# Last feed forward: three projections on rows without the norm's root, the root applied to their outcome

## The chip, the cores and the metric

One Trainium2 chip, one of its cores. The time is the device time of one execution in microseconds (us). Engines: TensorE (PE in the rows, its weight loads PEld), VectorE (DVE), ScalarE (ACT), GpSimd (POOL), and SyncE (SP), which only issues DMAs.

## What is computed

Two transformer blocks in a row on 512 tokens of width 1024, in float32. The change lies at the very end, in layer 1 of the second block, between its attention and its last feed forward:

```
yx = ob.transpose(1, 0, 2, 3).reshape(B, S, H * Dh) @ wo            # attention's output projection
x = x + g_x * rmsnorm(yx, norm_g[i, 1])                             # post norm
fx = rmsnorm(x, norm_g[i, 2]) * (1.0 + scf_x) + shf_x               # norm ahead of the feed forward
x = x + gf_x * rmsnorm(swiglu(fx, ffn_w1[i], ffn_w3[i], ffn_w2[i]), norm_g[i, 3])

def rmsnorm(x, g):      x * rsqrt(mean(x * x) + EPS) * g            # the mean is over the 1024 features
def swiglu(h, w1, w3, w2):  (silu(h @ w1) * (h @ w3)) @ w2          # 2816 hidden features
```

`scf_x` (scale) and `shf_x` (shift) are vectors of 1024, the same for all tokens.

## The kernel before

Activations lie transposed: 128 features on the partitions, 512 tokens along the row, so a width of 1024 is `KD` = 8 chunks (`X[:, c, :]`). Each product is made of three float32r matmuls of a high and a low half (`three`, lines 443 to 445): Wh x Hh, Wh x Hl, Wl x Hh. A projection to 128 features is one "slab" of weights (1024 x 128, 512 KB) and 8 x 3 = 24 matmuls of 512 columns into one PSUM bank.

A slab goes through four hands. SyncE loads it into one of three `raw` buffers (L2719), once the low half of the slab three places earlier is done. ScalarE copies it into `Wh` (L2137), once the slab three places earlier has been used. Another engine subtracts to make `Wl`: VectorE (L1344), or GpSimd (L2647) for the slabs that `by_pool` names, all of the first block. ScalarE and VectorE do this inside `ahead(key)`, which prepares all slabs up to two behind `key`. Engines run their queues strictly in order, so what stands ahead of an `ahead` in the code delays it.

The stretch in question runs so:

- `gqa_attend`: eight slabs `wo2`. The sums of squares of their outcome `Y2` give the root of the post norm, per token, in a tiny tile `small`. `token_rows` transposes it to a row (L589), with keep-warm matmuls around it (L651: float32 matmuls whose outcome nobody reads, `fill_in` gives their numbers, 1 and 4).
- `post_norm`: for each chunk VectorE scales `Y2` by gain and root (L1441) and adds it to `X` (L1512). ScalarE squares the new `X` (L2172), TensorE sums the squares over the partitions with a float32 matmul against ones (`norm_stat`, L565), eight times, and eight keep-warm matmuls follow.
- `norm_to_h`: ScalarE takes logarithm and exponential (L2185, L2188), VectorE refines the root with four operations (`rstd`, L1414, L1417, L1419, L1423; the result is `stat_r`, called `SR`), and then for each chunk VectorE scales `X` by gain and root (L1441), ScalarE adds the shift and writes the high half `Hh` (L2210), VectorE writes the low half `Hl` (L1458).
- `ffn_2`: for f = 0 to 10, and later 11 to 21, the projections `up1` and `up3` of hidden chunk f. The first two run together, chunk by chunk as `Hl` appears (`linear_pair`); the others one after the other (`linear`). ScalarE takes SiLU of up1 out of PSUM into `sl` (L2157), VectorE multiplies by up3 (L1673), ScalarE writes the high half `g_h` (L2307), VectorE the low half `g_l` (L1500). After 11 of them come the down projections.

In the text the projections are numbered in the order in which TensorE does them: up1 f=0, up3 f=0, up1 f=1, up3 f=1 (the fourth), up1 f=2 (the fifth).

Of the kernel before, what the change touches and what calls it, by code (L numbers as in the profile page):

```python
# [24 lines left out]
P = 128  # L25
# [69 lines left out]
def write(nc, a, out, tally):  # L95
# [197 lines left out]
    Y2 = at("Y2", 32, [KD, SEQ])  # L293
    XT = nc.alloc_sbuf_tensor_at("XT", [P, QT, D], F32, offset=int(hl_base - 16 * KB))
# [88 lines left out]
    WARM = 8  # L383

    def by_pool(key):

        return key[0] in BLOCK_1_SLABS or key[0:2] == ("dn", 1)
# [18 lines left out]
    def _(pe):  # L406
# [50 lines left out]
        def linear(job, key, src, n):  # L457
# [4 lines left out]
            gemm(job, w, Hh, Hl, n).then_inc(*fill(job))  # L462
            release[key] = full(job)
            mods()
# [91 lines left out]

        def stat(job, parts, n, matrix="ones"):
# [80 lines left out]
        WARM_AFTER = {("n1", 0): WARM, ("ln", "c"): 4, ("f", 0, "c"): 4, ("n", 1, "c"): 4, ("f", 1, "x"): WARM}  # L638
# [139 lines left out]
        def ffn_2(l, s):  # L778

            n, tag = NS[s], ("f", l, s)  # L780
            for half in range(2):
                for f in range(half * FH, (half + 1) * FH):
                    w = {x: a["ffn_w%s_2" % x][l, :, f * P:(f + 1) * P] for x in "13"}
                    if f == 0:
                        linear_pair(tag, n, *((("up" + x, l, s, f), w[x], "split") for x in "13"))
                    else:
                        for x in "13":
                            linear(("up" + x, l, s, f), ("up" + x, l, s, f), w[x], n)
# [374 lines left out]
        def gqa_attend():  # L1163
# [63 lines left out]
            token_rows(("post", ("att", "x")), fill_in=(1, 4))  # L1227
# [64 lines left out]
        pre(("f", 1, "x"), SEQ)  # L1292
# [23 lines left out]
    def _(dve):  # L1316
# [343 lines left out]

        def ffn_2(l, s):
            n, tag = NS[s], ("f", l, s)
            name = ("dn", 2, l, s)
            norm_to_h(tag, n, lambda c: col(2, l, s, 7, c), lambda c: col(2, l, s, 3, c))
            for half in range(2):
                for f in range(half * FH, (half + 1) * FH):
                    u1, u3 = ("up1", l, s, f), ("up3", l, s, f)
                    ahead(u1)
                    ahead(u3)
                    dve.wait_ge(*free(u1))  # L1670
                    dve.wait_ge(*full(u3))
                    i, o = tmp((name, f))
                    dve.tensor_tensor(o[:, 0:n], sl[f % 2][:, 0:n], bank(u3, n), ALU.mult).then_inc(*empty(u3))  # L1673
# [440 lines left out]
        post_norm(("att", "x"), SEQ, Y2, lambda c: col(2, 1, "x", 8, c))  # L2114
# [3 lines left out]
    def _(act):  # L2118
# [190 lines left out]
        def ffn_2(l, s):  # L2309
            n, tag, name = NS[s], ("f", l, s), ("dn", 2, l, s)  # L2310
            norm_to_h(tag, n, lambda c: col(2, l, s, 3, c))
            for half in range(2):
                for f in range(half * FH, (half + 1) * FH):
                    u1, u3 = ("up1", l, s, f), ("up3", l, s, f)
                    ahead(u1)
                    if f >= 2:
                        act.wait_ge(*free(("up3", l, s, f - 2)))
                    evict(u1, sl[f % 2][:, 0:n], n, ACT.Silu)
                    ahead(u3)
                    act.wait_ge(*free(u3))  # L2320
# [313 lines left out]
        squares_of_x(("f", 1, "x"), SEQ, lambda c: ready("x_new", ("att", "x"), c))  # L2634
# [183 lines left out]
```

## Time and profile before

| | us |
|---|---|
| median of 3 runs | 3263.64 |
| lowest and highest | 3260.55, 3272.95 |
| profiled execution | 3269.63 |
| its span in the trace | 3267.7 |
| TensorE busy in it | 3154.4 (97%) |
| VectorE, ScalarE, GpSimd busy | 1568.1, 1185.1, 817.0 |

The span is the trace's own; the profiled execution's time is 1.9 us more. Times in the rows count from the start of the span. The stretch that the change touches lies between 2866 and about 2911.

### The profile page before, as it was taken

How to read it: one execution, taken by the hardware profiler on the slowest of the kernel's cores; microseconds unless marked ns; L12 is line 12 of the kernel's file. 1: busy time of each engine (PE TensorE's matmuls, PEld its weight loads, DVE VectorE, ACT ScalarE, POOL GpSimd, SP SyncE). 2: the span in 40 equal slices, each digit the busy share in tenths (PEclk: the TensorE clock that was granted, in tenths of full speed). 3: DMA queues.
4: the chain of work that ended last, by engine and by line, in shares of the span. 5: the costliest groups of instructions: out<-in, count | busy, mean ns of one | idle time of the engine just before them, and what ended most of it. 6: DMA issues, size and time to landing. Idle time of an engine off the chain costs nothing.

```text
span 3267.7 us, 38743 instructions
## 1 busy us (share of the span) xinstructions
PE 3154.4 (97%) x15600; PEld 2489.3 (76%) x15600; DVE 1568.1 (48%) x2210; ACT 1185.1 (36%) x1764; POOL 817.0 (25%) x401
## 2 busy tenths in 40 slices
PE   6999999999999999999999899999999979999998
PEld 4657778887665777778877678888888658878887
DVE  3572146465366113334289754322334889653234
ACT  3443234243453224324331343121112558632223
POOL 4302436565330433344411000000000039400000
PEclk9999999999999999999999899999999989999999
DMA  6413426755430555463335212212221110122332
GB/s 238 126 46 109 139 88 191 227 181 179 123 118 12 161 178 170 149 192 91 94 97 131 54 49 61 65 60 64 65 65 52 43 35 1 40 71 87 107 89 79
DMA packets 429894, 337.23 MB, mean 103 GB/s; under 512 B 16638, under 2 KB 411224, under 8 KB 417429
## 3 DMA queue, kind: packets, MB, share of 16 engines
q1 hardware_dynamic: 427888, 333.42, 33.3%
q8 instruction: 125, 2.05, 0.3%
q10 hardware_dynamic: 580, 0.88, 0.1%
q0 software_dynamic: 1248, 0.46, 0.1%
q14 instruction: 53, 0.43, 0.0%
HBM read 319.58 MB, written 2.10 MB: 98 GB/s over the span
## 4 chain that ended last, share of the span: by engine, by line
PE 62%; DVE 5%; issue 1%; ACT 1%; SPq 0%; DMA 0%; ACTq 0%; POOL 0%; DVEq 0%
PE PS L443 18%; PE PS L444 17%; PE PS L445 17%; PE PS L902 1%; PE PS L577 1%; PE PS L1206 1%; PE PS L651 1%; PE PS L565 1%; PE PS L1175 1%; PE PS L696 1%; PE PS L1207 1%; PE PS L1186 1%; DVE X L1512 0%; PE PS L1176 0%; DVE q_parts L1783 0%
## 5 line engine op out<-in xcount | busy, mean ns | idle before, releaser
L443 PE MATMUL PS<-Hh,Wh 128*128 128x512 f32 x2208 | 875.4, 396 | 7.8 <-DVE Hl L1458 7.8
L2647 POOL TENSOR_TENSOR Wl<-raw,Wh 128x1024 fp32r<-128x1024 f32 (+2 forms) x254 | 617.2, 2438 | 992.5 <-ACT Wh L2137 992.5
L444 PE MATMUL PS<-Hl,Wh 128*128 128x512 f32 x2208 | 861.8, 390 | 0.0
L445 PE MATMUL PS<-Hh,Wl 128*128 128x512 f32 x2208 | 861.1, 390 | 0.0
L2137 ACT ACTIVATE Wh<-raw 128x1024 fp32r<-128x1024 f32 (+2 forms) x442 | 435.9, 987 | 394.0 <-PE PS L445 346.8
L443 PEld LDWEIGHTS PS<-Hh,Wh 128*128 128x128 f32 x2208 | 415.7, 188 | 115.7 <-issue 50.5
L445 PEld LDWEIGHTS PS<-Hh,Wl 128*128 128x128 f32 x2208 | 415.7, 188 | 87.5
L444 PEld LDWEIGHTS PS<-Hl,Wh 128*128 128x128 f32 x2208 | 416.1, 188 | 69.0 <-issue 3.7
L1344 DVE TENSOR_TENSOR Wl<-raw,Wh 128x1024 fp32r<-128x1024 f32 (+3 forms) x188 | 217.5, 1157 | 380.6 <-ACT Wh L2137 380.1
L2042 DVE SCALAR_TENSOR_TENSOR cv<-PS,vcols,cv 128x510 f32<-128x510 f32 (+1 forms) x176 | 123.7, 745 | 216.9 <-ACT cv L2566 216.9
L443 PE MATMUL PS<-g_h,Wh 128*128 128x512 f32 x528 | 206.6, 391 | 3.5 <-POOL Wl L2647 3.5
L2679 POOL CAST k_hi<-k_ctx 64x512 fp32r<-64x512 f32 x4 | 4.2, 1042 | 806.2 <-DVE k_ctx L1441 806.0
L445 PE MATMUL PS<-g_h,Wl 128*128 128x512 f32 x528 | 205.5, 389 | 0.0
L444 PE MATMUL PS<-g_l,Wh 128*128 128x512 f32 x528 | 205.5, 389 | 0.0
L444 PE MATMUL PS<-hc_l,Wh 128*128 128x256 f32 x576 | 161.9, 281 | 0.0
L445 PE MATMUL PS<-hc_h,Wl 128*128 128x256 f32 x576 | 161.8, 281 | 0.0
L443 PE MATMUL PS<-hc_h,Wh 128*128 128x256 f32 x576 | 161.8, 281 | 0.0
L2694 POOL TENSOR_SCALAR p<-p,small 128x768 f32<-128x768 f32 x64 | 140.4, 2214 | 49.7 <-DVE small L2094 49.7
L2566 ACT ACTIVATE cv<-PS,vcols 128x512 f32<-128x512 f32 x88 | 68.6, 780 | 192.2 <-PE PS L445 188.8
L565 PE MATMUL PS<-sq,cst 128*128 128x512 f32 (+2 forms) x196 | 100.4, 627 | 26.5 <-DVE stat_v L1414 16.2
L443 PEld LDWEIGHTS PS<-hc_h,Wh 128*128 128x128 f32 x576 | 108.1, 188 | 19.7
L444 PEld LDWEIGHTS PS<-hc_l,Wh 128*128 128x128 f32 x576 | 108.1, 188 | 19.7
(390 smaller groups left out, 4806.1 us busy)
## 6 DMA issues: line engine op xcount, KB each, us to landing
raw<-in_ffn_w SPq DMA_DIRECT2D x108, 512.0 KB, 3.6
mod_w<-in_w_mod SPq DMA_DIRECT2D x48, 1024.0 KB, 4.9
raw<-in_w_up SPq DMA_DIRECT2D x88, 512.0 KB, 4.7
mod_w<-in_w_ada SPq DMA_DIRECT2D x40, 1024.0 KB, 4.8
raw<-in_w_in SPq DMA_DIRECT2D x62, 512.0 KB, 3.9
raw<-in_w_down SPq DMA_DIRECT2D x32, 384.0 KB, 4.9
raw<-in_conv_w_pw SPq DMA_DIRECT2D x24, 512.0 KB, 4.1
UQ<-U SPq DMA_DIRECT2D x112, 99.4 KB, 2.2
```

The lines of the kernel that those rows point to most:

```text
L443: pe.matmul(o, wh, xh, start=start, stop=False, skip_group_check=True)
L444: pe.matmul(o, wh, xl, start=False, stop=False, skip_group_check=True)
L445: return pe.matmul(o, wl, xh, start=False, stop=stop, skip_group_check=True)
L565: mm = pe.matmul(bank(job, n), const(matrix)[lo:hi, :], SQ[i][lo:hi, 0:n], start=first, stop=final, skip_group_check=True)
L577: mm = pe.matmul(PS[:, bank_of[job], t:t + 1], part[:, t * P:(t + 1) * P], const("ones", 0, 1), start=first and t == 0, stop=final, skip_g ...
L651: pe.matmul(PS[:, b, :], const("ident"), cst[:, 0:512], start=True, stop=True)
L1344: dve.tensor_tensor(low, src, high.bitcast(F32), ALU.subtract).then_inc(*mark("w_low", k))
L2042: ins = dve.scalar_tensor_tensor(o, bank(ups[s])[:, 0:SEQ - lag], vec(("w_conv", l), tap * 2 * FC + s * FC + f), o, ALU.mult, ALU.add)
L2137: act.activation(high, src, ACT.Copy).then_inc(*mark("w_high", k))
L2566: act.activation(cv[f % 2][s][:, :], bank(job), ACT.Identity, bias=vec(("b_conv", l), s * FC + f), scale=vec(("w_conv", l), 2 * 2 * FC + s ...
L2647: pool.tensor_tensor(low, src, high.bitcast(F32), ALU.subtract).then_inc(*mark("w_low_pool", one[0]))
L2694: pool.tensor_scalar(p2[n % 5][:, :], p2[n % 5][:, :], ri2[n % 5], None, ALU.mult)\
```

## The change

Three slabs are "late": up1 f=0, up3 f=0, up1 f=1. They no longer read `Hh` and `Hl`, but `late_h` and `late_l`, the halves of x times gain without root and shift. The root is one factor per token, so it can be applied to the outcome; the shift's share is one number per hidden feature, which 24 one-column matmuls of the raw weights against the shift vector give. The fourth and all later projections read `Hh` and `Hl` as before, the fourth chunk by chunk. The low halves of the slabs of the third, fourth and fifth projection are made by GpSimd. `post_norm_late` is `post_norm` with the late low half two chunks behind.

The diff, cut to its core, in the order TensorE (`linear_late`), VectorE (`post_norm_late` and the first `ffn_2`), ScalarE (the second `ffn_2`), GpSimd, SyncE (the wait ahead of the fourth projection's load):

```diff
+    LATE = ("up1", 1, "x", 0), ("up3", 1, "x", 0), ("up1", 1, "x", 1)
+    LATE_LOWS = ("up1", 1, "x", 1), ("up3", 1, "x", 1), ("up1", 1, "x", 2)
     def by_pool(key):
-        return key[0] in BLOCK_1_SLABS or key[0:2] == ("dn", 1)
+        return key[0] in BLOCK_1_SLABS or key[0:2] == ("dn", 1) or key in LATE_LOWS
...
+        def linear_late(tag, srcs):
...
+            for m, job in enumerate(LATE):
+                r = (first + m) % RAW
+                pe.wait_ge(*ready("raw_in%d" % r, job))
+                for i in range(KD):
+                    mm = pe.matmul(PS[:, bank_of[shift], m:m + 1], raw[r][:, i * P:(i + 1) * P],
+                                   MOD[2, 1][:, 3 * KD + i, 0:1], start=(m, i) == (0, 0), stop=i == KD - 1,
+                                   skip_group_check=True)
+            mm.then_inc(*fill(shift))
...
+            for i in range(KD):
+                norm_stat(tag, i, n)
+                pe.wait_ge(*ready("late_low", tag, i))
+                for job, w in zip(LATE, ws):
+                    mm = products(job, w, i)
...
+            job, w = LATE[2], slab(LATE[2], k_p(srcs[2]), KD, P)
+            for i in range(KD):
+                mm = products(job, w, i)
...
-        WARM_AFTER = {("n1", 0): WARM, ("ln", "c"): 4, ("f", 0, "c"): 4, ("n", 1, "c"): 4, ("f", 1, "x"): WARM}
+        WARM_AFTER = {("n1", 0): WARM, ("ln", "c"): 4, ("f", 0, "c"): 4, ("n", 1, "c"): 4}
...
-            token_rows(("post", ("att", "x")), fill_in=(1, 4))
+            token_rows(("post", ("att", "x")), fill_in=(1, 1))
-        pre(("f", 1, "x"), SEQ)
...
+        def post_norm_late(tag, post, n, src, gg, g):
...
+            def low(c):
+                dve.wait_ge(*ready("late_high", tag, c))
+                dve.scalar_tensor_tensor(late_l[c][:, 0:n], x[:, c, 0:n], g(c), late_h[:, c, 0:n].bitcast(F32),
+                                         ALU.mult, ALU.subtract).then_inc(*mark("late_low", tag, c))
...
         def ffn_2(l, s):
...
+            dve.wait_ge(*full(("shift", tag)))
+            dve.tensor_copy(shift_out, PS[:, bank_of["shift", tag], 0:3]).then_inc(*empty(("shift", tag)))
...
+                    if u1 in LATE:
+                        dve.wait_ge(*full(u1))
+                        dve.tensor_tensor(late_o[:, 0:n], bank(u1, n), SR[:, 0:n], ALU.mult).then_inc(*empty(u1))
...
+                    if u3 in LATE:
...
+                        dve.scalar_tensor_tensor(o[:, 0:n], late_o[:, 0:n], shift_out[:, 1:2], sl[f % 2][:, 0:n],
+                                                 ALU.add, ALU.mult).then_inc(*mark("late_gate", f))
...
         def ffn_2(l, s):
...
-            norm_to_h(tag, n, lambda c: col(2, l, s, 3, c))
+            ahead(first_slab(tag))
+            for c in range(KD):
+                act.wait_ge(*ready("x_new", ("att", "x"), c))
+                act.activation(late_h[:, c, :], X[:, c, :], ACT.Identity, scale=DER[2, l][:, KD + c, 0:1])\
+                   .then_inc(*mark("late_high", tag, c))
+                square((tag, c), X[:, c, 0:n], n)
+            root(("ss", tag), n)
+            ahead(LATE[1])
...
+            norm_highs(tag, n, lambda c: col(2, l, s, 3, c))
...
+                    if u1 in LATE:
+                        act.wait_ge(*free(u1))
+                        silu(sl[f % 2][:, 0:n], tb(("late", u1))[:, 0:n], bias=shift_out[:, 2 * f:2 * f + 1])\
+                            .then_inc(*mark("late_silu", f))
...
+        for key in LATE_LOWS:
...
+            pool.wait_ge(*ready("w_high", key))
+            pool.tensor_tensor(low, src, high.bitcast(F32), ALU.subtract).then_inc(*mark("w_low_pool", key))
...
+                if slabs[n - RAW][0] == LATE[0]:
+                    sp.wait_ge(*full(("shift", LATE_TAG)))
```

TensorE, from the transposes of the post norm's root on, before:

```order
L589 MATMUL PS<-cst,small 128x128 x4
L651 MATMUL PS<-cst 128x512 x4
L565 MATMUL PS<-sq0,cst 128x512
L565 MATMUL PS<-sq1,cst 128x512
...
L651 MATMUL PS<-cst 128x512 x8
L443 MATMUL PS<-Hh,Wh0 128x512
L444 MATMUL PS<-Hl,Wh0 128x512
```

and now (L694 and L632 are the old L651 and L589, L608 the old L565, L451 to L453 the old L443 to L445):

```order
L632 MATMUL PS<-cst,small 128x128 x4
L694 MATMUL PS<-cst 128x512
L577 MATMUL PS<-mod2_1,raw0 128x1 x8
L577 MATMUL PS<-mod2_1,raw1 128x1 x8
L577 MATMUL PS<-mod2_1,raw2 128x1 x8
L608 MATMUL PS<-sq0,cst 128x512
L451 MATMUL PS<-late_h_159,Wh0 128x512
L452 MATMUL PS<-late_l0_160,Wh0 128x512
L453 MATMUL PS<-late_h_159,Wl0 128x512
L451 MATMUL PS<-late_h_159,Wh1 128x512
L452 MATMUL PS<-late_l0_160,Wh1 128x512
L453 MATMUL PS<-late_h_159,Wl1 128x512
```

Eleven keep-warm matmuls are gone, 24 one-column ones are there, and each statistic is followed by six products.

ScalarE, from the end of the norm's highs on (`Wh1` behind `g_h` is the fifth projection's weights in both), before:

```order
L2210 ACTIVATE Hh<-tmp0,mod2_1 128x512
L2157 ACT_TABLE_LOAD
L2157 ACTIVATE sl0_118<-PS 128x512
L2137 ACTIVATE Wh0<-raw0 128x1024
L2307 ACTIVATE g_h_112<-tmp1 128x512
L2137 ACTIVATE Wh1<-raw1 128x1024
L2157 ACTIVATE sl1_119<-PS 128x512
```

and now:

```order
L2301 ACTIVATE Hh<-tmp0,mod2_1 128x512
L2241 ACT_TABLE_LOAD
L2241 ACTIVATE sl0_118<-tmp1,mod_row_52 128x512
L2398 ACTIVATE g_h_112<-tmp0 128x512
L2228 ACTIVATE Wh1<-raw1 128x1024
L2241 ACTIVATE sl1_119<-tmp1,mod_row_52 128x512
```

The fourth projection's weights (`Wh0`) have moved ahead of the highs; the fifth's stand where they stood, behind `g_h`.

VectorE, from the end of the norm's lows on, before:

```order
L1458 SCALAR_TENSOR_TENSOR Hl<-tmp0,mod2_1,Hh 128x512
L1344 TENSOR_TENSOR Wl2<-raw2,Wh2 128x1024
L1344 TENSOR_TENSOR Wl0<-raw0,Wh0 128x1024
L1673 TENSOR_TENSOR tmp1<-sl0_118,PS 128x512
L1500 TENSOR_TENSOR g_l_113<-tmp1,g_h_112 128x512
```

and now (`mod_row` holds the shift's share):

```order
L1501 SCALAR_TENSOR_TENSOR Hl<-tmp0,mod2_1,Hh 128x512
L1739 COPY mod_row_52<-PS 128x3
L1748 TENSOR_TENSOR tmp1<-PS,stat_r 128x512
L1754 TENSOR_TENSOR tmp2<-PS,stat_r 128x512
L1760 SCALAR_TENSOR_TENSOR tmp0<-tmp2,mod_row_52,sl0_118 128x512
L1543 TENSOR_TENSOR g_l_113<-tmp0,g_h_112 128x512
```

Three low halves of weights have gone to GpSimd, and a copy, the products with the root and a gate that adds the shift's share have come.

## Rows read from the trace of the kernel before

**Rows 1.** The page's chain that ended last, shares of the span by engine.

```profile
PE 62%; DVE 5%; issue 1%; ACT 1%; SPq 0%; DMA 0%; ACTq 0%; POOL 0%; DVEq 0%
```

**Rows 2.** Busy times by stretch: length, PE, PEld, DVE, ACT, POOL; clock; DMA.

```profile
2870.00:2880.00 10.00, 9.46 (x20) 3.01 (x18) 9.97 (x16) 4.15 (x7) 0.00 (x0) 1.00 0.00 0
...
2900.00:2912.00 12.00, 12.00 (x55) 9.93 (x54) 5.66 (x6) 4.33 (x7) 0.00 (x0) 1.00 0.57 166
```

**Rows 3.** TensorE's timeline: start, us, line, out<-in, count [idle before]; two rows per float32 matmul.

```profile
2866.06 0.95 PE L577 MATMUL PS<-cst,stat_v 128*128 128x1 f32 x8
2866.91 1.05 PE L577 MATMUL PS<-cst,sq 128*128 128x1 f32 x8
...
2869.76 3.60 PE L651 MATMUL PS<-cst 128*128 128x512 f32 x8
2873.20 9.10 PE L565 MATMUL PS<-sq,cst 128*128 128x512 f32 x16
2882.13 7.03 PE L651 MATMUL PS<-cst 128*128 128x512 f32 x16
2888.60 0.79 PE L443 MATMUL PS<-Hh,Wh 128*128 128x512 f32 x1
...
2910.56 0.39 PE L445 MATMUL PS<-Hh,Wl 128*128 128x512 f32 x1
2910.78 0.39 PE L443 MATMUL PS<-Hh,Wh 128*128 128x512 f32 x1
```

**Rows 4.** VectorE's timeline in the same stretch.

```profile
2870.03 1.41 DVE L1441 SCALAR_TENSOR_TENSOR tmp<-Y,der,PS 128x512 f32<-128x512 f32 x2 [0.87 <-PE PS L589]
2871.35 0.69 DVE L1512 TENSOR_TENSOR X<-X,tmp 128x512 f32<-128x512 f32 x1
...
2887.57 0.75 DVE L1458 SCALAR_TENSOR_TENSOR Hl<-tmp,mod,Hh 128x512 fp32r<-128x512 f32 x1 [0.19 <-ACT Hh L2210]
...
2897.07 1.22 DVE L1344 TENSOR_TENSOR Wl<-raw,Wh 128x1024 fp32r<-128x1024 f32 x1
...
2902.15 0.68 DVE L1673 TENSOR_TENSOR tmp<-sl,PS 128x512 f32<-128x512 f32 x1
```

**Rows 5.** ScalarE's timeline in the same stretch.

```profile
2872.07 0.63 ACT L2172 ACTIVATE sq<-X 128x512 f32<-128x512 f32 x1 [3.57 <-DVE X L1512]
...
2882.33 0.69 ACT L2185 ACTIVATE stat_y<-PS,cst 128x512 f32<-128x512 f32 x1 [1.43 <-PE PS L565]
...
2883.59 1.04 ACT L2137 ACTIVATE Wh<-raw 128x1024 fp32r<-128x1024 f32 x1
...
2902.86 0.63 ACT L2307 ACTIVATE g_h<-tmp 128x512 fp32r<-128x512 f32 x1 [1.89 <-DVE tmp L1673]
2903.40 1.04 ACT L2137 ACTIVATE Wh<-raw 128x1024 fp32r<-128x1024 f32 x1
```

**Rows 6.** Timeline of GpSimd and VectorE in the first block, a low half alone last.

```profile
126.65 2.74 POOL L2647 TENSOR_TENSOR Wl<-raw,Wh 128x1024 fp32r<-128x1024 f32 x1 [5.71 <-ACT Wh L2137]
...
127.18 2.77 DVE L1423 SCALAR_TENSOR_TENSOR stat_r<-stat_t,stat_y 128x512 f32<-128x512 f32 x1
...
1080.61 2.39 POOL L2647 TENSOR_TENSOR Wl<-raw,Wh 128x1024 fp32r<-128x1024 f32 x1 [4.23 <-ACT Wh L2137]
```

**Rows 7.** The page's DMA issues of feed forward slabs: count, size, median us to landing.

```profile
raw<-in_ffn_w SPq DMA_DIRECT2D x108, 512.0 KB, 3.6
```

**Rows 8.** Busy times by stretch again, two places where the clock fell.

```profile
46.00:50.00 4.00, 4.00 (x12) 3.10 (x12) 4.00 (x7) 2.20 (x4) 0.00 (x0) 0.58 0.10 29
...
1844.00:1848.00 4.00, 4.00 (x25) 4.00 (x24) 4.00 (x10) 1.89 (x3) 0.00 (x0) 0.59 0.00 0
```

**Rows 9.** TensorE's timeline at these two places.

```profile
44.76 0.77 PE L443 MATMUL PS<-Hh,Wh 128*128 128x512 f32 x1 [5.25 <-DVE Hl L1458]
...
49.71 0.40 PE L443 MATMUL PS<-Hh,Wh 128*128 128x512 f32 x1
...
1843.21 17.07 PE L577 MATMUL PS<-cst,sq 128*128 128x1 f32 x85 [1.10 <-ACT sq L2172]
```

More of the change, by code:

```diff
@@ L455, in gemm, with linear @@
             return mm
-        def linear(job, key, src, n):
+        def linear(job, key, src, n, each=None):
             begin(job)
@@ L461, in linear @@
             tally.h_reader[0] = job
-            gemm(job, w, Hh, Hl, n).then_inc(*fill(job))
+            gemm(job, w, Hh, Hl, n, each=each).then_inc(*fill(job))
             release[key] = full(job)
@@ L784, in ffn_2 @@
                     if f == 0:
[L785 removed]
+                        linear_late(tag, [w["1"], w["3"], a["ffn_w1_2"][l, :, P:2 * P]])
                     else:
[L787 to L788 removed]
+                        for x in "13"[f == 1:]:
+                            linear(("up" + x, l, s, f), ("up" + x, l, s, f), w[x], n,
+                                   each=(lambda i: ready("h_low", tag, i)) if f == 1 else None)
                 down(("dn", 2, l, s), a["ffn_w2_2"][l], half, n, None, last_turns)
@@ L1659, in ffn_both, with add @@
             post_norms(("ffn", 0), 0, 9)
+        def post_norm_late(tag, post, n, src, gg, g):
+            row, x, pending = ("r", ("post", post)), X, []
+            dve.wait_ge(*full(row))
+            def add(c, i, t):
+                dve.wait_ge(*t)
+                tmp_free[i] = after(dve.tensor_tensor(x[:, c, 0:n], x[:, c, 0:n], TMP[i][:, 0:n], ALU.add),
+                                    "x_new", post, c)
+            def low(c):
+                dve.wait_ge(*ready("late_high", tag, c))
+                dve.scalar_tensor_tensor(late_l[c][:, 0:n], x[:, c, 0:n], g(c), late_h[:, c, 0:n].bitcast(F32),
+                                         ALU.mult, ALU.subtract).then_inc(*mark("late_low", tag, c))
+            for c in range(KD + 2):
+                if c < KD:
+                    i, o = tmp(("post", post, c))
+                    t = scaled(o[:, 0:n], src[:, c, 0:n], gg(c), n, r=bank(row, n))
+                    if c < KD - 1:
+                        t = own(t)
+                    else:
+                        t.then_inc(*empty(row))
+                        t = free(row)
+                    pending.append((c, i, t))
+                if 0 < c <= KD:
+                    add(*pending[c - 1])
+                if c > 1:
+                    low(c - 2)
         def ffn_2(l, s):
@@ L2695, in _ @@
                 .then_inc(*mark("p2_scaled", h, i))
+        for key in LATE_LOWS:
+            d = [one[0] for one in slabs].index(key)
+            src, high = halves(slabs[d], raw[d % RAW], Wh[d % WS])
+            _, low = halves(slabs[d], raw[d % RAW], Wl[d % WS])
+            pool.wait_ge(*ready("w_high", key))
+            pool.tensor_tensor(low, src, high.bitcast(F32), ALU.subtract).then_inc(*mark("w_low_pool", key))
     @block.sync
```

49 lines of the change are left out of this document (40 added, 9 removed).

## The prediction, made before the change was run

> **What bounds the kernel now.** I read the chain that ended last first [rows 1]: matmuls carry most of it, and VectorE is next. So a change pays only where TensorE waits or runs filler. The change touches one such place, the stretch between the attention's output projection and the fifth projection of the last feed forward; I read it in the busy times by stretch [rows 2] and then instruction by instruction. TensorE looks full there, but look at what it does [rows 3]: statistics and keep-warm matmuls (L651) fill it from 2869.76 to 2888.60. The first projection starts at 2888.60, when VectorE hands over the first low part. From then on nothing stops: four projections are 96 matmuls, the last of them issues at 2910.56, and the fifth projection starts at 2910.78, so a matmul of 512 columns costs 0.227 us and a projection 5.44. Everything behind the fifth projection is fed in time in both kernels, so the change is worth what it does to this 2910.78.
>
> **The change, part by part.**
>
> TensorE first. One keep-warm matmul remains after the row transposes instead of four: four take 3.44 us (2869.76 to 2873.20), so one ends at 2870.62 [rows 3]. Now 24 one-column matmuls for the shift follow. The nearest rows are the one-column ones of L577: eight trace rows in 0.85 us, and eight rows are four float32 matmuls (the program order says x4), so 0.213 us each and 5.1 us for 24. They end at 2875.8 (rounded up for the change of form). The first statistic would be ready at about 2873.4: ScalarE's first square starts at 2872.07 [rows 5], and the new high part, 0.6 to 0.7, goes ahead of it. So the shift's matmuls are exposed by 2.4 us.
>
> Then come eight rounds of one statistic, 0.86 (the price of a float32 matmul of 512 columns), and six products, 1.36: 2.22 us a round. VectorE's round is 0.66 + 0.60 + 0.66 = 1.9 us (row gain and sum in [rows 4], and a third operation of the form of L1458), ScalarE's two activations are 1.2, so TensorE sets the pace. The low part of chunk 0 is due at 2874.0, or 0.7 later if it meets GpSimd; TensorE wants it at 2876.7. The last statistic ends at T = 2875.8 + 7 x 2.22 + 0.86 = 2892.2. Before, T was 2882.13 (the next matmul's start in [rows 3]). T is 10.1 us later, and two projections lie ahead of it instead of behind. The third follows with no wait and ends at T + 1.36 + 5.44 = T + 6.8.
>
> The root and the eight chunks of the norm are the same work as before. From T to the end of the last low part it took 2897.07 - 2882.13 = 14.9 us [rows 3, 4]. What is new is GpSimd beside it. ScalarE converts the fourth projection's weights at the same point as before, 1.3 us behind its logarithm [rows 5]; the low half that follows is now GpSimd's. In [rows 6] such a low half started during L1419, and the next VectorE operation, the same L1423 with two SBUF operands, took 2.77 us instead of 0.69. The timing here would be the same within 0.2 us. I take the whole 2.08: the norm ends at T + 17.0. Bounds: 0 (no meeting) and 2.4 (a full GpSimd operation, [rows 6]).
>
> The fourth projection reads this norm chunk by chunk; chunk 0 comes at T + 8.3, chunk 7 at T + 17.1, and it ends at T + 17.9. TensorE works there half the time.
>
> Then the point on which the forecast turns. In the order of ScalarE, the conversion of the fifth projection's weights stands behind sl0 and g_h of f = 0, and these wait for VectorE, which does them only when its norm is over. Before, that conversion began at 2903.40 [rows 5] and with VectorE's low half (1.2) was done five microseconds early. Now the chain from the end of the norm is: shift copy 0.3, product with the root 0.7, SiLU 0.65, gate 0.7 to 0.75 (with the waits between them 2.45 up to the start of g_h), g_h 0.54 and the conversion 1.05 [rows 5], GpSimd's low half 0.1 + 2.39 [rows 6], and 0.1 to the matmul: 6.6 us. On VectorE a low half took 1.2; on GpSimd it is twice that. The fifth projection starts at T + 17.0 + 6.6 = T + 23.6 = 2915.8 against 2910.78: **5.0 us later**. TensorE stands still for 5.7 us ahead of it.
>
> No other queue comes into it. SyncE holds the fourth projection's load until the shift's matmuls are over (2875.8), and the two loads queued behind it wait too; three loads of 3.6 us [rows 7] end by about 2887, and the first is wanted at T + 1.5. The eight VectorE operations added in the post norm (5.3 us) are covered by TensorE's slower round; that cover is 0.3 us a chunk and would cost 0.3 x 8 if it were gone. The three scalings by the root and the SiLU on a scaled copy are in the chain above for f = 0 and behind the fifth projection's matmuls for f = 1.
>
> **The clock.** Two new places look like ones where the granted clock fell. First, one-column matmuls: at 1843.21 a long row of them starts right behind 512-column work; in 1844 to 1848 the clock is 0.59 though TensorE is busy all the time [rows 8, 9], which is a mix of 2.4 and 1.2 GHz. Here 5.2 us of them come behind a stretch that is already thin. I take 5 us at 1.2 GHz, which cost half, 2.5 us (bounds 0 and 3.4); T and all behind it move by that. The Trainium skill ("TensorE: Matmul & The Clock Gate", section "Why this matters for your kernels") says otherwise: it advises to keep TensorE continuously busy to have the full clock, and by that the one-column matmuls, issued without a gap, would protect it. By the skill's rule the term is 0 and the sum 2.5 us lower; the trace does not agree, since the rows show the clock falling in a full queue. Second, the pause of 5.7 us: behind one of 5.25 us, twelve matmuls took 4.95 us (44.76 to 49.71) instead of 2.7, and the clock of 46 to 50 is 0.58 [rows 8, 9]. That is 2.2 us (bounds 1.5 and 3.4).
>
> **Sum:** 5.0 + 2.5 + 2.2 = 9.7 us slower. The profiled execution took 3269.63 us (span 3267.7), so its like would be 3279.3; it stood 6.0 above the median of the runs shown, which gives 3263.64 + 9.7 = **3273.3 us**. That is 0.3%. About 0.5% (16.3 us) is what a measurement of this kernel can tell from no change, so I call it the same, with the sign on the slow side.
>
> **Rivals.** (1) The clock holds through one or both places. For it: TensorE has had fillers in this stretch with the clock at 1.00 throughout [rows 2]. Against it: [rows 8, 9]. Time: +5.0 to +7.5, 3268.6 to 3271.1. (2) The early part is cheap: the one-column matmuls end before the first square is ready (they would have to take under 0.12 us each), which gives 2.4 back, the clock stays up, and GpSimd and VectorE do not meet, another 2.1: 5.0 - 4.5 = +0.5, 3264.1. Only if GpSimd's low half were as quick as VectorE's besides (1.2 less) would the change be ahead, by 0.7 us. For it: the new form has no row of its own, and the square of chunk 0 could come later than I say, behind its high part. Against it: each of the terms has a row. The change's own aim, projections ahead of the root, is limited by the fourth projection in any case: it cannot end before the norm does, T + 15.8. With the cheap T of 2889.8 that is 2905.6, a gain of 5 us if the fifth projection's weights were ready, which the order excludes. (3) Slower beyond 0.5%: the clock stays at 1.2 GHz for long. The thin stretch begins at 2866, the half-busy fourth projection and the pause follow, and in the one-column stretch of [rows 9] (17 us) the clock did not come back while it lasted. If it stayed low from the shift's matmuls to behind the pause, the dense rounds would run at half speed. It decides from (16.3 - 5.0) x 2 = 23 us of dense work at 1.2 GHz; for 26 us it gives +18, 3282. Against it: eight rounds of six full products are dense, and after the pause at 44.76 the full clock was back at 49.71.
>
> **How the numbers follow.** The forecast as summed, between +7.5 and +13: 0.62. Rival 1: 0.20. Rival 2, with any smaller time, gains included: 0.09. Rival 3: 0.09. Unknown costs from their bounds give -2.1 to +0.3 (port), -2.5 to +0.9 (first clock term), -0.7 to +1.2 (second); the runs before lie from 3260.55 to 3272.95, so a median can move by 4 for no reason. From rival 1 less that to the forecast's upper end plus that: 3264 to 3284. I take 3263 to 3284. Faster by over 0.5% would need more than the whole stretch holds: 0.01. Slower by over 0.5% is rival 3: 0.09. The rest, 0.90, lies within.
>
> **What the changed profile would show.** 24 one-column matmuls (48 rows) from about 2870.6, over 5 us long; rounds of 2.2 us; the last statistic at about 2892 to 2895; L1466 (stat_r) at about 2.8 us beside GpSimd's low half; the fourth projection in eight pieces 1.3 us apart; a pause of nearly 6 us ended by GpSimd's Wl; the fifth projection 23.6 us behind the last statistic; and a granted clock under 1 in two places. I am wrong if the fifth projection starts before 2911, if the pause is not there, if L1466 stays at 0.69, or if the clock stays at 1.00 from 2870 to 2920.

## The result, and the profile after

The changed kernel took **3275.65 us** (median of 20 runs, 3269.96 to 3284.09), the kernel before 3264.95 us on the same chip (20 runs, 3259.91 to 3273.09). The medians differ by 10.7 us. The ratio is 1.0029 with a 95% interval of 1.002 to 1.0039, which is a cost of 6.5 to 12.7 us. The forecast was 9.7 us and 3273.3 us.

The page barely shows it. The chain that ended last is the one of [rows 1] with a point moved from VectorE to issue:

```profile
PE 62%; DVE 4%; issue 2%; ACT 1%; SPq 0%; DMA 0%; POOL 0%; ACTq 0%; POOLq 0%; DVEq 0%
```

The profiled execution took 3271.65 us (span 3269.8), only 2.0 more than the one before. The rest lies ahead of the change: this execution reached the token sums that open the touched stretch at 2857.62, the one before at 2866.06 [rows 3], 8.4 us later, though the program is the same up to there. So totals of single executions say nothing here, and I count everything from the start of these token sums. Seen from there, the product that VectorE forms behind the sixth projection (the gate of f = 2, the first step that both kernels have alike) starts at 66.39 us in the changed kernel and at 55.86 in the one before: **10.53 us later**. The next ones are 10.2, 10.5 and 10.5 later. The whole loss is in this stretch: from the token sums to the end of the span it is 412.2 us against 401.7, the same 10.5 that the gate shows. 10.53 - 8.44 = 2.1 is what the two profiled executions differ by (2.0), and 10.53 lies within the interval of the timing.

TensorE's timeline in the stretch (start and length in us, count, idle before in brackets), to be laid beside [rows 3]:

```profile
2862.18 5.50 PE L577 MATMUL PS<-mod,raw 128*128 128x1 f32 x48
2867.55 2.06 PE L608 MATMUL PS<-sq,cst 128*128 128x512 f32 x2
...
2873.68 1.02 PE L608 MATMUL PS<-sq,cst 128*128 128x512 f32 x2
...
2875.92 1.02 PE L608 MATMUL PS<-sq,cst 128*128 128x512 f32 x2
```

```profile
2894.18 0.47 PE L451 MATMUL PS<-Hh,Wh 128*128 128x512 f32 x1 [1.40 <-DVE Hl L1501]
...
2910.55 0.79 PE L451 MATMUL PS<-Hh,Wh 128*128 128x512 f32 x1 [6.67 <-POOL Wl L2806]
2911.14 0.63 PE L452 MATMUL PS<-Hl,Wh 128*128 128x512 f32 x1
2911.57 0.63 PE L453 MATMUL PS<-Hh,Wl 128*128 128x512 f32 x1
```

The first row is the shift's share, 24 matmuls of one column in 5.37 us. Behind it come the eight rounds, 2.24 us from one statistic (L608) to the next. The first of them reads 2.06 instead of 1.02. Then the fourth projection in eight pieces, and the row to look at longest: the fifth projection starts at 2910.55, after 6.67 us in which TensorE does nothing, released by GpSimd's low half. Its first matmuls take 0.63 instead of the 0.39 of [rows 3].

Busy times by stretch (columns as in [rows 2]: PE, PEld, DVE, ACT, POOL; clock; DMA):

```profile
2866.00:2871.00 5.00, 5.00 (x22) 3.63 (x22) 5.00 (x9) 2.49 (x5) 0.00 (x0) 0.66 0.40 116
2871.00:2886.00 15.00, 15.00 (x55) 9.95 (x53) 6.81 (x11) 5.65 (x10) 0.00 (x0) 1.00 0.22 67
...
2906.00:2910.00 4.00, 0.00 (x0) 0.00 (x0) 1.76 (x3) 3.03 (x4) 1.85 (x1) 0.79 0.01 2
2910.00:2914.00 4.00, 3.45 (x8) 2.77 (x9) 2.80 (x4) 1.79 (x3) 0.50 (x1) 0.50 0.53 154
2914.00:2918.00 4.00, 4.00 (x16) 3.21 (x16) 1.04 (x1) 0.00 (x0) 0.00 (x0) 0.86 0.79 231
```

The clock fell twice, as in [rows 8]: once while TensorE was busy all the time (first row; 0.66 over 5 us is 3.4 us at 1.2 GHz), and once in the pause and on into the fifth projection (0.50 from 2910 to 2914).

What TensorE waited for stands in the timelines of VectorE, ScalarE and GpSimd, which answer [rows 4 to 6]:

```profile
2888.87 2.77 DVE L1466 SCALAR_TENSOR_TENSOR stat_r<-stat_t,stat_y 128x512 f32<-128x512 f32 x1
...
2901.23 1.63 DVE L1501 SCALAR_TENSOR_TENSOR Hl<-tmp,mod,Hh 128x512 fp32r<-128x512 f32 x2
2902.78 0.15 DVE L1739 COPY mod_row<-PS 128x3 f32<-128x3 f32 x1
2902.85 0.68 DVE L1748 TENSOR_TENSOR tmp<-PS,stat_r 128x512 f32<-128x512 f32 x1
...
2905.71 0.75 DVE L1760 SCALAR_TENSOR_TENSOR tmp<-tmp,mod_row,sl 128x512 f32<-128x512 f32 x1 [1.59 <-ACT sl L2241]
```

```profile
2885.97 0.69 ACT L2276 ACTIVATE stat_y<-PS,cst 128x512 f32<-128x512 f32 x1 [3.86 <-PE PS L608]
...
2903.61 1.28 ACT L2241 ACT_TABLE_LOAD   x1 [1.53 <-DVE tmp L1748]
2904.90 0.72 ACT L2241 ACTIVATE sl<-tmp,mod_row 128x512 f32<-128x512 f32 x1
2906.50 0.63 ACT L2398 ACTIVATE g_h<-tmp 128x512 fp32r<-128x512 f32 x1 [0.88 <-DVE tmp L1760]
2907.03 1.04 ACT L2228 ACTIVATE Wh<-raw 128x1024 fp32r<-128x1024 f32 x1
```

```profile
2888.34 2.74 POOL L2806 TENSOR_TENSOR Wl<-raw,Wh 128x1024 fp32r<-128x1024 f32 x1 [24.90 <-ACT Wh L2228]
2908.15 2.35 POOL L2806 TENSOR_TENSOR Wl<-raw,Wh 128x1024 fp32r<-128x1024 f32 x1 [17.06 <-ACT Wh L2228]
```

Read the last four rows of ScalarE and the second of GpSimd as one chain: product with the root at 2902.85, **table load at 2903.61**, SiLU, gate, g_h, conversion, low half, and TensorE at 2910.55. The load is the one link that the prediction doesn't have. In the kernel before, the same load runs ahead of any wait, three microseconds before its SiLU's products are there:

```profile
2896.39 1.28 ACT L2157 ACT_TABLE_LOAD   x1
2899.43 0.60 ACT L2157 ACTIVATE sl<-PS 128x512 f32<-128x512 f32 x1 [1.76 <-PE PS L445]
```

A product of VectorE ahead of the SiLU isn't enough to hold the load. In the first block of the changed kernel the load ran ahead of such a wait:

```profile
473.10 1.28 ACT L2241 ACT_TABLE_LOAD   x1
474.56 0.63 ACT L2241 ACTIVATE sl<-cv 128x512 f32<-128x512 f32 x1 [0.17 <-DVE cv L2133]
```

The code has one wait in front of the SiLU at both of these places, and two at 2903.61 (for the shift copy and for the product). That the second wait is what keeps the load behind fits these rows, but no run tests it.

### The profile page after: what moved, and what is told of

It reads as the page before. It is cut to its first block, busy times and chain, and to the rows that moved or that the text cites. A ratio compares the mean times of both kernels' runs of the same rounds, so it can differ in the third digit from the quotient of the medians.

```text
span 3269.8 us, 38816 instructions
## 1 busy us (share of the span) xinstructions
PE 3143.6 (96%) x15626; PEld 2484.2 (76%) x15626; DVE 1575.0 (48%) x2219; ACT 1190.6 (36%) x1772; POOL 824.9 (25%) x404
## 4 chain that ended last, share of the span: by engine, by line
PE 62%; DVE 4%; issue 2%; ACT 1%; SPq 0%; DMA 0%; POOL 0%; ACTq 0%; POOLq 0%; DVEq 0%
PE PS L451 17%; PE PS L452 17%; PE PS L453 17%; PE PS L946 1%; PE PS L620 1%; PE PS L1250 1%; PE PS L1219 1%; PE PS L739 1%; PE PS L608 1%; PE PS L1251 1%; PE PS L1230 1%; PE PS L694 1%; PE PS L1220 0%; DVE q_parts L1874 0%; DVE both_tmp L1484 0%
## 5 line engine op out<-in xcount | busy, mean ns | idle before, releaser
L451 PE MATMUL PS<-Hh,Wh 128*128 128x512 f32 x2184 | 867.1, 397 | 18.2 <-DVE Hl L1501 11.4
L452 PE MATMUL PS<-Hl,Wh 128*128 128x512 f32 x2184 | 852.8, 390 | 0.0
L453 PE MATMUL PS<-Hh,Wl 128*128 128x512 f32 x2184 | 852.4, 390 | 0.0
L451 PEld LDWEIGHTS PS<-Hh,Wh 128*128 128x128 f32 x2184 | 411.6, 188 | 128.6 <-issue 52.5
L453 PEld LDWEIGHTS PS<-Hh,Wl 128*128 128x128 f32 x2184 | 411.3, 188 | 87.2
L451 PE MATMUL PS<-g_h,Wh 128*128 128x512 f32 x528 | 206.7, 391 | 3.5 <-POOL Wl L2752 3.5
L453 PE MATMUL PS<-g_h,Wl 128*128 128x512 f32 x528 | 205.5, 389 | 0.0
L453 PE MATMUL PS<-hc_h,Wl 128*128 128x256 f32 x576 | 161.8, 281 | 0.0
L451 PE MATMUL PS<-hc_h,Wh 128*128 128x256 f32 x576 | 161.8, 281 | 0.0
L2799 POOL TENSOR_SCALAR p<-p,small 128x768 f32<-128x768 f32 x64 | 140.7, 2220 | 49.7 <-DVE small L2185 49.7
L608 PE MATMUL PS<-sq,cst 128*128 128x512 f32 (+2 forms) x196 | 98.0, 606 | 26.8 <-DVE stat_v L1457 16.2
L451 PEld LDWEIGHTS PS<-hc_h,Wh 128*128 128x128 f32 x576 | 108.1, 188 | 19.7
```

What stands on the lines that cost most here:

```text
L451: pe.matmul(o, wh, xh, start=start, stop=False, skip_group_check=True)
L452: pe.matmul(o, wh, xl, start=False, stop=False, skip_group_check=True)
L453: return pe.matmul(o, wl, xh, start=False, stop=stop, skip_group_check=True)
L608: mm = pe.matmul(bank(job, n), const(matrix)[lo:hi, :], SQ[i][lo:hi, 0:n], start=first, stop=final, skip_group_check=True)
L2799: pool.tensor_scalar(p2[n % 5][:, :], p2[n % 5][:, :], ri2[n % 5], None, ALU.mult)\
```

## The experiments

Two theories stood at the start. **Mine:** four separate costs make up the 10.5 us, which are the shift's matmuls with the clock that they bring down, GpSimd's low half in VectorE's way, the chain from the norm's end to the fifth projection's weights (with the table load in it), and the clock behind the pause. **The rival:** one of them makes the others (the pause is there anyway, since the sixth projection or the norm ends last), so that mending one moves nothing. All numbers of this table are from the traces, in us from the start of the token sums; "log" is the start of the post norm's logarithm (L2276), which starts 0.2 behind the last statistic, "gate" the gate of f = 2.

| kernel | log | root's widest operation | fifth projection | gate | log to gate | half clock ahead of log / at the fifth or sixth |
|---|---|---|---|---|---|---|
| before | 16.27 | 0.69 | 44.72 | 55.86 | 39.6 | none / none |
| changed | 28.35 | 2.77 | 52.93 | 66.39 | 38.0 | 3.4 / 6.8 |
| table load early | 29.98 | 2.77 | 53.28 | 66.27 | 36.3 | 6.8 / 6.8 |
| filler in the pause | 29.94 | 2.76 | 54.60 | 65.88 | 35.9 | 6.8 / none |
| narrow low half | 31.57 | 0.83 | 54.21 | 67.18 | 35.6 | 10.2 / 6.8 |
| fifth's weights early | 28.34 | 2.77 | 48.1 | 63.42 | 35.1 | 3.4 / 3.4 |
| 3 of 24 shift matmuls | 24.65 | 2.77 | 49.24 | 62.72 | 38.1 | none / 6.8 |
| shift matmuls spread | 27.97 | 2.77 | 52.57 | 66.10 | 38.1 | none / 6.8 |
| four queue edits | 28.34 | 0.69 | 45.49 | 56.90 | 28.6 | 3.4 / none |
| the same, spread 9 + 15 | 27.96 | 0.69 | 45.11 | 56.50 | 28.5 | none / none |
| the same, spread 15 + 9 | 26.67 | 0.69 | 43.83 | 55.21 | 28.5 | none / none |

The stretch ahead of the logarithm and the one behind it hang on different things, and the length of the first half clock changed from run to run of the same code (below). So an edit behind the logarithm is read from the column "log to gate". The totals of the single executions (3271.2 to 3276.1 us for the first four variants, 3280.0, 3283.2 and 3274.0 for the next three) are not used: the latter three had reached the token sums only at 2869.6, 2869.6 and 2868.7, 11 to 12 us later than the changed kernel, ahead of any edit.

**The table load ahead of the wait.** ScalarE loads the SiLU table before it waits for VectorE's product:

```diff
+                        if table_set[0] != SILU:
+                            act.preload_act_table_set(SILU)
+                            table_set[0] = SILU
                         act.wait_ge(*free(u1))
```

> The change with one edit: ScalarE loads the SiLU table before it waits for VectorE's product with the root, not after it. All times from the start of the post norm's one-column sums. In the changed kernel the fifth projection starts at 52.9 us and the gate of f = 2 (the end of the sixth projection) runs at 66.4 (before the change: 44.7 and 55.9). Theory A (the fifth projection's weights wait behind VectorE's norm and ScalarE's sl0 and g_h, so every step of that chain counts): the load of 1.28 us lies in the chain, and hiding it gives 1.1 to 1.3: fifth at 51.7, gate at 65.2. Theory B (the late root alone sets the time, and the chain has slack): no change, 52.9 and 66.4.

The load ran beside the norm's last chunk, and the pause became shorter by its length (ScalarE's and TensorE's timelines):

```profile
2902.81 1.28 ACT L2420 ACT_TABLE_LOAD   x1
2904.34 0.72 ACT L2241 ACTIVATE sl<-tmp,mod_row 128x512 f32<-128x512 f32 x1 [0.25 <-DVE tmp L1748]
```

```profile
2909.99 0.80 PE L451 MATMUL PS<-Hh,Wh 128*128 128x512 f32 x1 [5.39 <-POOL Wl L2809]
```

5.39 instead of 6.67: the load costs 1.28 us, all of its length, in the chain. From the logarithm to the gate it is 1.75: the second half clock reached 3.5 us into the fifth projection here and 4.6 in the changed kernel, which is the other 0.5. The Trainium skill ("ScalarE: Activation LUTs", section "Step-by-step: what each stage is for") says that the compiler places such a load right before the activation that needs it; this trace agrees, and here that place is behind the wait, while in the kernel before it was ahead of it (2896.39 and 2899.43 above). (The section "What ACT_TABLE_LOAD costs" gives about 1283 ns for the load, as measured here, and 1380 ns of drain besides, which isn't in these rows: the SiLU follows the load at once, and taking the load away gave 1.28 and not 2.7.)

**Filler in the pause.** Six keep-warm matmuls ahead of the fifth projection:

```diff
+                            if f == 1 and x == "3":
+                                keep_warm(6)
```

> The change with six keep-warm matmuls (5.2 us) between the fourth and the fifth projection, where TensorE stands still for 6.7 us. Theory A (the pause makes the clock fall, and that costs 2.3 us of the fifth projection): the fifth still starts at 52.9, its matmuls run at 2.4 GHz, the gate of f = 2 comes 2.2 us earlier, at 64.2. Rival (the clock falls because of what was ahead: the half-busy fourth projection, or at random): clock under 1 in the fifth projection all the same, gate at 66.4.

The idle time ahead of the fifth projection fell to 1.61 us and its matmuls ran at full clock:

```profile
2913.00:2918.00 5.00, 4.95 (x22) 4.14 (x23) 3.51 (x4) 1.58 (x2) 0.00 (x0) 1.00 0.71 208
```

The fifth projection started no earlier (24.66 behind the logarithm, 24.58 in the changed kernel), and the gate was 2.1 us nearer. That is the price of the second half clock, forecast at 2.2.

**A narrow low half.** GpSimd makes only 128 of the 1024 columns of the fourth projection's low half (the rest is left out):

```diff
-            pool.tensor_tensor(low, src, high.bitcast(F32), ALU.subtract)
+            cols = slice(0, P) if key == LATE_LOWS[1] else slice(0, 8 * P)
+            pool.tensor_tensor(low[:, cols], src[:, cols], high[:, cols].bitcast(F32), ALU.subtract)
```

> The change with GpSimd's low half of the fourth projection's weights made for 128 of 1024 columns only (the rest is left out, so the fourth projection is computed with old low halves there). Theory A (GpSimd's operation blocks VectorE's stat_r, 2.77 instead of 0.69 us): stat_r at 0.7 to 1.0, the norm and with it the fifth projection 1.8 to 2.1 us earlier, at 50.9, gate of f = 2 at 64.4. Rival (VectorE's operation is long by itself, or waits for ScalarE): stat_r stays near 2.8, nothing moves.

```profile
2893.99 0.83 DVE L1466 SCALAR_TENSOR_TENSOR stat_r<-stat_t,stat_y 128x512 f32<-128x512 f32 x1
```

```profile
2893.46 0.82 POOL L2807 TENSOR_TENSOR Wl<-raw,Wh 128x128 fp32r<-128x128 f32 x1 [28.13 <-ACT Wh L2228]
```

VectorE's operation was 0.83 beside a short GpSimd operation and 2.77 beside a long one, with the same operands: it waits for GpSimd to end. The fifth projection came 1.94 us nearer to the logarithm, and the pause stayed 6.67, so this cost (2.08 forecast) adds to the pause and isn't part of it. (The gate came 2.4 us nearer. The other 0.5 is again the second half clock, which reached 3.6 us into the fifth projection instead of 4.6.) The Trainium skill ("SBUF — State Buffer", section "SBUF: two separate sides") has this as a lock that whichever of the two starts first holds for its whole instruction. The rows agree: GpSimd's 2888.34 + 2.74 is 2891.08, and VectorE's operation, put at 2888.87, ended at 2891.64, a normal operation's 0.6 behind that.

**The fifth projection's weights early.** ScalarE converts them right behind the logarithm, where the fourth's are converted:

```diff
-            ahead(LATE[1])
+            ahead(LATE[2])
```

> The change with the conversion of the fifth projection's weights moved on ScalarE from behind g_h of f = 0 to ahead of the norm's highs, next to the fourth's. Theory A (this place in ScalarE's order makes the pause; GpSimd's second low half now blocks one more VectorE operation for about 2.4 us): pause gone, fifth at 48.4, straight behind the fourth, no fall of the clock there, gate of f = 2 at 59.5. The same without a second block: 46.0 and 57.1. Theory B (the late root alone): the fifth stays at 52.9.

The fifth projection came where I had it, right behind the fourth. The gate was four microseconds later than expected, for the next row of TensorE's timeline is a new wait:

```profile
2917.79 0.39 PE L453 MATMUL PS<-Hh,Wl 128*128 128x512 f32 x1
2920.48 0.47 PE L451 MATMUL PS<-Hh,Wh 128*128 128x512 f32 x1 [2.30 <-DVE Wl L1387]
```

The sixth projection's conversion now stood where the fifth's had, behind sl1 on ScalarE (2918.03), and TensorE waited for that with another half clock behind it. And GpSimd made two low halves in a row, which held VectorE twice:

```profile
2895.21 5.53 POOL L2806 TENSOR_TENSOR Wl<-raw,Wh 128x1024 fp32r<-128x1024 f32 x2 [24.89 <-ACT Wh L2228]
```

```profile
2895.74 2.77 DVE L1466 SCALAR_TENSOR_TENSOR stat_r<-stat_t,stat_y 128x512 f32<-128x512 f32 x1
2898.55 3.40 DVE L1484 SCALAR_TENSOR_TENSOR tmp<-X,der,stat_r 128x512 f32<-128x512 f32 x2
```

So the rival holds in part: the gate gained 2.9 us (35.1 behind the logarithm instead of 38.0), and the rest of the wait went to the next conversion in the line.

**Three of the 24 one-column matmuls.** The loop over the chunks runs for the last one only:

```diff
-                for i in range(KD):
+                for i in range(KD - 1, KD):
```

> Of the 24 one-column matmuls for the shift's share only the last chunk's 3 are left (the rest of the share is not computed). Times here are from the start of the token sums. In the changed kernel the fifth float32 row of filler and the 24 matmuls were followed by 3.41 us at the half clock, and the post norm's logarithm began at 28.35 (29.9 in two variants in which the half clock lasted 6.83 us). My theory: the full queue of one-column matmuls makes the clock fall and they are exposed by about 2.4 us; with 3 of them both are gone: no stretch of half clock before the post norm, logarithm at about 24.0 (28.35 - 2.4 - 1.9). Rival: the clock falls anyway, for the thin work of the token sums and the filler ahead of them, and the matmuls cost only their exposure: half clock is still there near 9 to 10, logarithm at 25.7 or later. The rest of the stretch moves with the logarithm: fifth projection 24.6 behind it by both.

The half clock ahead of the logarithm was gone, and TensorE waited 2.50 us for the first square:

```profile
2874.20 0.72 PE L577 MATMUL PS<-mod,raw 128*128 128x1 f32 x6
2877.43 1.10 PE L608 MATMUL PS<-sq,cst 128*128 128x512 f32 x2 [2.50 <-ACT sq L2263]
```

The logarithm came at 24.65 (24.0 expected): 3.7 us earlier. If 1.7 of it is the clock (3.4 us at half of it), 2.0 is left for the time by which 21 matmuls ran past the first square. Behind the logarithm nothing changed (38.1).

**The same 24, spread.** 9 ahead of the rounds, 3 behind each of five rounds:

```diff
-                for i in range(KD):
-                    mm = pe.matmul(PS[:, bank_of[shift], m:m + 1], raw[r][:, i * P:(i + 1) * P],
+            def shifts(i):
+                for m in range(3):
+                    mm = pe.matmul(PS[:, bank_of[shift], m:m + 1], raw[(first + m) % RAW][:, i * P:(i + 1) * P],
...
+            for i in range(3):
+                shifts(i)
...
+                if i + 3 < KD:
+                    shifts(i + 3)
```

> The same 24 one-column matmuls, but 9 ahead of the eight rounds and 3 behind the statistic and the products of each of the first five rounds; nothing is left out. My theory: it is the unbroken row of them that makes the clock fall, so the half clock of 3.41 or 6.83 us near 9.7 is gone (1.7 to 3.2 us), the logarithm begins at about 26.6 instead of 28.35, and the rounds that carry three more are 0.65 us longer than the others (2.24). Rival: their number is what counts, or the thin work around them: half clock near 9 to 11 stays, logarithm at 28.3 or 30.

No half clock, as expected; but the logarithm came at 27.97 and not at 26.6. The expected 26.6 is 28.35 less the clock's 1.7, with the matmuls exposed no more than before (2.0 us). But the fifteen in the rounds cost their full length, 5 x 0.67 = 3.3 us on top of the 24.65 with three, since TensorE sets the pace of the rounds; and 1.16 us ahead of the first square stayed empty.

**Four queue edits together.** VectorE makes the low halves of the fourth and fifth projections (right behind the root and right behind the norm), ScalarE converts the fifth's weights ahead of the norm and the sixth's behind its last high part, and loads the table early:

```diff
-    LATE_LOWS = ("up1", 1, "x", 1), ("up3", 1, "x", 1), ("up1", 1, "x", 2)
+    LATE_LOWS = (("up1", 1, "x", 1),)
...
-            norm_to_h(tag, n, lambda c: col(2, l, s, 7, c), lambda c: col(2, l, s, 3, c))
+            rstd(("ss", tag), n, D)
+            ahead(LATE[1])
+            norm_to_h(tag, n, lambda c: col(2, l, s, 7, c), lambda c: col(2, l, s, 3, c), rooted=True)
+            ahead(LATE[2])
...
-            ahead(LATE[1])
+            ahead(LATE[2])
...
+            ahead(("up3", l, s, 1))
```

> Four edits of the queues, nothing of the computation: VectorE in place of GpSimd makes the low halves of the fourth projection (right behind the root) and of the fifth (right behind the norm); ScalarE converts the fifth's weights ahead of the norm's last steps and the sixth's behind them; and ScalarE loads the SiLU table ahead of its wait for VectorE's product. My theory: each wait that the four looks so far found has gone and no other takes its place: the widest operation of the root is 0.7 instead of 2.77, the norm is shorter by 2.1 less the 1.2 of the low half that VectorE now makes in it, the fifth projection begins about 17.3 behind the logarithm (24.58 in the changed kernel), the sixth follows without the 2.30 that it waited in the look before, and the gate of f = 2 starts about 28.3 behind the logarithm (38.0). With the logarithm at 28.3 to 30 that is 56.6 to 58.3 behind the token sums (66.4 in the changed kernel, 55.9 in the one before). Rival: a new wait comes up, on the bank of the third f's products or on VectorE's queue, and the gate stays 33 or more behind the logarithm, near the 35.1 of the early fifth.

From the logarithm to the gate it was 28.56 us (28.3 expected, 38.0 in the changed kernel): 9.5 us are mended by these four edits. The second half clock is gone with the pause, and no new wait came up: the longest on TensorE from the fourth projection to the gate is 0.50 us. The four were not taken apart here. TensorE's row at the fifth projection:

```profile
2914.16 0.49 PE L451 MATMUL PS<-Hh,Wh 128*128 128x512 f32 x1 [0.17 <-DVE Wl L1387]
```

**The edits and the spread together**, timed against the kernel before:

> The four edits of the queues and the spread one-column matmuls together. By my theory it keeps the change's idea and loses what cost it: logarithm at 26.6, gate of f = 2 at 54.8 behind the token sums against 55.9 in the kernel before, so a time 1 us below before, 3264 (3260 to 3268), which is the same by any measurement of this size, and some 10 us below the changed kernel. Rival A: the clock falls all the same, 1.7 to 3.3 us more, time 1 to 3 us above before. Rival B: the sum of the change is not in this stretch at all but in the program's other parts, whose instructions the change moved; then the time stays near 3275 whatever is mended here.

3267.87 us (median of 12 runs) against 3268.39, ratio 0.9998 with an interval of 0.9984 to 1.0012. The gate came at 56.50; I had it at 54.8, and 1.4 of the difference is the error of the spread above. So what the change cost is gone, and rival B with it: from the token sums to the end of the span this trace has 402.8 us, the kernel before 401.7 and the changed one 412.2, and the time is not near the 3275 of rival B. A second timing, with the split of the 24 matmuls moved by one number:

```diff
-            for i in range(3):
+            for i in range(5):
                 shifts(i)
...
-                if i + 3 < KD:
-                    shifts(i + 3)
+                if i + 5 < KD:
+                    shifts(i + 5)
```

> The last kernel with one number changed: 15 of the 24 one-column matmuls stand ahead of the eight rounds instead of 9, and 3 behind each of the first three rounds instead of five. With 9 ahead TensorE still waited 1.16 us for the first square, and the 15 in the rounds cost 0.67 us for each three, all of it exposed (3.3 us). My theory: six more fill that pause (6 x 0.224 = 1.34), so 1.2 us are gained: the logarithm at 26.8 instead of 27.96 behind the token sums, gate of f = 2 at 55.3 against 55.9 in the kernel before and 56.5 in the last one. For the clock there are two cases: it holds, since 15 in a row are fewer than 24, and then the numbers above stand; or it falls as behind the 24 (3.41 or 6.83 us), which costs 1.7 to 3.2: logarithm at 28.5 or 30, gate at 57 or 58.5. Time: 3267 or 3269 by the median of the kernel before of 3268.4, not to be told from it in any case.

```profile
2866.22 3.40 PE L579 MATMUL PS<-mod,raw 128*128 128x1 f32 x30
2869.48 1.10 PE L615 MATMUL PS<-sq,cst 128*128 128x512 f32 x2
```

```profile
2866.00:2871.00 5.00, 5.00 (x36) 4.21 (x35) 5.00 (x8) 2.48 (x4) 1.48 (x1) 1.00 0.00 0
2871.00:2876.00 5.00, 5.00 (x28) 3.85 (x26) 5.00 (x9) 3.21 (x5) 0.00 (x0) 1.00 0.01 3
```

Fifteen in a row filled the wait, the clock stayed at 1.00, the logarithm came at 26.67 (26.8 expected) and the gate at 55.21 (55.3), 0.65 us ahead of the kernel before. Timed, it is 3264.16 us against 3262.76, ratio 1.0003 with an interval of 0.9989 to 1.0017: the same. 0.65 us are 0.02%, far below what the runs can tell.

## Why the prediction was right, point by point

**The fifth projection's start, +5.0 forecast.** Counted from the token sums the prediction put it at 49.7 (2915.8 - 2866.1), and with its first clock term at 52.2; it came at 52.93. The parts of it:

- The shift's matmuls: 5.1 us forecast, 5.37 measured. Their exposure: 2.4 forecast; the run with three of them gives 2.0.
- The round: 2.22 forecast, 2.24 measured. TensorE sets its pace, as said; the spread showed that this holds to the point that every matmul added to a round is exposed.
- From the last statistic to the end of the norm: T + 17.0 forecast, 17.0 measured (2885.77 to 2902.8), with the root's L1466 at 2.77 as said.
- From there to the fifth projection: 6.6 forecast, 7.75 measured. **This is the step that was wrong.** "SiLU 0.65" left out the table load of 1.28 us in front of it. The row was in the trace of before, but there it stood ahead of the wait, beside VectorE's work, and I took its place for given. In the changed kernel it stands behind the wait for VectorE's product with the root. Why it does here, and didn't ahead of other waits, is open (see the rows of 473.10 above).

**The first clock term, +2.5 forecast.** 1.7 in the profiled execution (3.4 us at 1.2 GHz). The variants of the same code show 3.4 or 6.8 us, so 1.7 or 3.4: the forecast lies between what came out. The mechanism was right: the clock fell in a full queue. That the size came near is in part luck, since it was not the same in two executions of the same code. The Trainium skill ("TensorE: Matmul & The Clock Gate", section "Why this matters for your kernels") advises continuous work to have the full clock; for work of this kind the traces do not agree.

**The second clock term, +2.2 forecast.** The fifth projection's first twelve matmuls took 4.99 us instead of 2.7, which is 2.3, and the filler in the pause gave 2.1 back.

**The sum.** 8.21 (52.93 - 44.72) and 2.3 are 10.5 us, against 9.7. The chain missed 1.15 (the load, less a tenth elsewhere), the first clock term was 0.8 too large, and the rest is 0.5 too short in tenths of the shift's row, the rounds and the second clock term. Two of the errors cancelled in part, so the total is nearer than its worst step.

**The signs of being wrong.** The pause was there, L1466 took 2.77 us and the clock fell. The first sign, a fifth projection before 2911, came by its letter: it started at 2910.55. But this execution had reached the token sums 8.44 us earlier, and 2910.55 + 8.44 is 2919.0, so the sign should have been counted from a mark inside the execution.

**The rivals.** Rival 1, the clock holds: wrong for this kernel, though three variants that issue all 24 matmuls show that it can hold ahead of the logarithm. Rival 2, the early part is cheap: none of its three conditions came. Rival 3, the clock stays low for long: the longest stretch was 6.8 us. What I called the order's exclusion in rival 2 ("if the fifth projection's weights were ready") turned out to matter most, though the 5 us that I gave it were not there. With the weights ready, the clock up and the root undisturbed, the best version is ahead by 0.65 us. The reason can be read in the table. The idea shortens the way from the logarithm to the gate by 11.1 us (39.6 to 28.5), since two projections are done by then and the third runs beside the root. It lengthens the way to the logarithm by 10.4 (16.27 to 26.67), since these projections and the shift's matmuls stand where filler stood and the statistics wait for them in the rounds. And in the 17.2 us from the logarithm to the fifth projection, in which the norm and the fifth's low half are made, TensorE has 53 matmuls to do (the end of the last round, the third and the fourth projection), which would be 12.0 us in a dense row: the fourth goes at the pace at which VectorE hands over the chunks, 1.32 us each where its matmuls need 0.68.

## What to carry to other kernels

When work is moved ahead of a wait, write out, engine by engine, what then stands behind that wait: here a table load, a conversion and a low half stood behind one product of VectorE and made a pause of 6.7 us. Moving the load alone gave back its own length, and moving the conversion alone handed part of the wait to the next conversion. Work put in place of filler isn't free if the engine that ran the filler sets the pace of what follows. And compare single executions from a mark just ahead of the changed place: here that showed 10.5 us where the totals of two profiles differed by 2.0.

## What the runs showed of the hardware

- The granted clock fell behind an unbroken row of 24 one-column matmuls in each of the six traces that have one (to 1.2 GHz, for 3.4 us in three of them and for 6.8 in the other three), and it did not in the four traces with 3, 9 (twice) or 15 in a row. TensorE was busy all through the 24, while the traces with 3 and with 9 had an idle gap of 2.50 or 1.16 us in the same place. So it wasn't idleness that brought it down. Unbroken rows are not the only cause, though: the trace of the narrow low half has 3.4 us of half clock from 3.1 us on, ahead of its row, beside the token sums and filler, and three traces have 3.4 us of it during the half-busy fourth projection, where the matmuls waited for VectorE anyway and no cost shows. The longer case behind the row, in the run with the table load early:

```profile
2866.00:2873.00 7.00, 7.00 (x18) 4.63 (x19) 6.12 (x10) 1.96 (x3) 0.00 (x0) 0.53 0.63 190
```

- What decides between 3.4 and 6.8 us in the same code is open. It moved the logarithm by 1.6 us from run to run.
- Executions of kernels that are alike up to there reach the token sums up to 13 us apart (2856.7 to 2869.6 over these traces), ahead of any edit. This goes with the half clock granted until then: 82 to 92 us of it in the four traces that arrive by 2859.6, 99 in the one at 2861.7, 109 to 126 in the six from 2864.5 on. One such place is a row of eight sums of squares with 256 columns each, the same code and the same 2.78 us of waiting ahead of it in the kernel before (clock 0.79 from 1950 to 1966) and in the changed one (1.00 from 1945 to 1961), 2 us longer in the first:

```profile
1954.72 6.88 PE L565 MATMUL PS<-sq,cst 128*128 128x256 f32 x16 [2.78 <-ACT sq L2172]
1950.02 4.90 PE L608 MATMUL PS<-sq,cst 128*128 128x256 f32 x16 [2.78 <-ACT sq L2263]
```

Why the clock falls in one execution and not in the other is open.
